# Attention with both heads of a pair together: scores in alternate row halves, values as weights of the sums, probabilities divided first

## The reference

```
def dilated_mixer(x, k_sh, v_sh, cos, sin, norm_g, w_q, q_norm_g, w_o):
    h = rms_norm(x, norm_g)
    q = (h @ w_q).reshape(Bn, Sn, N_GROUPS, HEADS_PER_GROUP, ATT_HEAD)
    q = apply_rope(rms_norm(q, q_norm_g[:, None, :]), cos, sin)
    for gi, (window, dilation) in enumerate(DILATED_GROUPS):
        o, l = dilated_window_attention(q[:, :, gi], k_sh[:, :, gi], v_sh[:, :, gi], window, dilation)
    ...
    alpha = jax.nn.softmax(jnp.stack(lses), axis=0)
    o = jnp.einsum('gbsh,gbshd->bshd', alpha, jnp.stack(outs))
    return o.reshape(Bn, Sn, O_WIDTH).astype(x.dtype) @ w_o
```

## Time and profile before

| | |
|---|---|
| median of 3 runs | 1139.49 us |
| lowest, highest | 1134.31, 1140.91 us |
| span of the profiled execution | 1131.1 us |
| TensorE, VectorE, ScalarE, GpSimd busy | 95%, 58%, 38%, 7% of the span |
| granted TensorE clock, mean | 0.975 |
| steps of the pairs in the trace | half 0 of pair 1 at 617.56 us, of pair 7 at 845.12, last step to 899.7 |
| DMA | 137.30 MB, mean 121 GB/s |

### The profile page before, as it was taken

One profiled execution on the slowest core, in us unless ns is written; L12 is line 12 of the kernel. 1 busy time (PEld: TensorE's weight loads), 2 busy tenths in 40 slices (PEclk: granted clock), 3 DMA queues, 4 the chain that ended last, 5 costly groups with the idle time before them and its releaser, 6 DMA issues.

```text
span 1131.1 us, 17783 instructions
## 1 busy us (share of the span) xinstructions
PE 1070.4 (95%) x6728; PEld 955.1 (84%) x6728; DVE 654.6 (58%) x1107; ACT 429.7 (38%) x643; POOL 78.4 (7%) x52
## 2 busy tenths in 40 slices
PE   5989999999998799999978999999999899999998
PEld 3779779789687699999968999999999638999997
DVE  6754654753764655455476766776677216555553
ACT  2311312321312443343244556655655503433431
POOL 0000000000000000000002211221122000000000
PEclk9989999999999899999989999999999898999999
DMA  9310050040130375676449444334432314766761
GB/s 291 116 48 1 1 160 1 11 148 1 40 110 1 94 218 173 183 199 174 129 129 288 120 132 139 111 113 137 139 111 74 112 37 139 196 167 191 196 170 56
DMA packets 194954, 137.30 MB, mean 121 GB/s; under 512 B 7261, under 2 KB 185949, under 8 KB 194794
## 3 DMA queue, kind: packets, MB, share of 16 engines
q1 hardware_dynamic: 194922, 136.85, 41.5%
HBM read 135.78 MB, written 1.05 MB: 121 GB/s over the span
## 4 chain that ended last, share of the span: by engine, by line
issue 55%; PE 36%; POOL 5%; DVE 2%; DMA 1%; ACT 1%; SPq 0%; POOLq 0%; DVEq 0%; ACTq 0%
PE bank L392 21%; PE wide L392 15%; POOL gsm L1448 5%; DMA ring<-in_w_kv 1%; DVE x L1045 0%; DVE wsp L1045 0%; DMA x<-in_x 0%; DVE fhn L1048 0%; POOL small L1448 0%; ACT once L798 0%; SPq L359 0%; DVE work L1045 0%; PE bank L402 0%; PE bank L744 0%; PE wide L402 0%
## 5 line engine op out<-in xcount | busy, mean ns | idle before, releaser
L392 PE MATMUL bank<-wpj,hkq 128*128 128x384 f32 x1152 | 217.2, 343 | 5.4 <-DVE wpj L1045 3.1
L392 PEld LDWEIGHTS bank<-wpj,hkq 128*128 128x128 f32 x1152 | 201.1, 190 | 12.0 <-issue 4.6
L1045 DVE TENSOR_TENSOR wsp<-ring,wsp 128x1024 fp32r<-128x1024 f32 (+1 forms) x88 | 151.0, 1756 | 34.0 <-ACT wsp L798 34.0
L798 ACT ACTIVATE wsp<-ring 128x1024 fp32r<-128x1024 f32 (+1 forms) x88 | 130.0, 1484 | 27.2 <-PE wide L392 27.2
L392 PEld LDWEIGHTS wide<-hsp,wsp 128*128 128x128 f32 x1056 | 133.2, 197 | 5.2 <-DVE hsp L1045 3.6
L392 PE MATMUL wide<-hsp,wsp 128*128 128x256 f32 x1056 | 134.1, 288 | 2.8 <-DVE hsp L1045 2.8
L392 PE MATMUL bank<-work 128*128 128x128 f32 (+4 forms) x896 | 130.6, 301 | 6.4 <-DVE work L1048 4.2
L392 PEld LDWEIGHTS bank<-hsp,wsp 128*128 128x128 f32 x1056 | 129.5, 192 | 1.6
L392 PE MATMUL bank<-hsp,wsp 128*128 128x256 f32 x1056 | 130.2, 283 | 0.0
L392 PEld LDWEIGHTS bank<-work 128*128 128x128 f32 (+2 forms) x896 | 117.0, 195 | 14.9 <-issue 5.8
L1448 POOL TENSOR_TENSOR gsm<-gsm,mhalf 128x6 f32<-128x6 f32 (+1 forms) x40 | 73.8, 1844 | 582.7 <-DVE gsm L1168 348.0
(11 more groups left out here) (155 smaller groups left out, 1197.8 us busy)
## 6 DMA issues: line engine op xcount, KB each, us to landing
ring<-in_f_w_gu SPq DMA_DIRECT2D x88, 512.0 KB, 5.6
ring<-in_w_kv SPq DMA_DIRECT2D x96, 256.0 KB, 3.3
ring<-in_f_w_down SPq DMA_DIRECT2D x44, 512.0 KB, 3.7
ring<-in_b_w_q SPq DMA_DIRECT2D x48, 256.0 KB, 3.5
wmix<-in_a_w_k SPq DMA_DIRECT2D x4, 1024.0 KB, 7.0
wmix<-in_a_w_r SPq DMA_DIRECT2D x4, 1024.0 KB, 10.3
wmix<-in_a_w_v SPq DMA_DIRECT2D x4, 1024.0 KB, 5.9
wmix<-in_a_w_o SPq DMA_DIRECT2D x4, 1024.0 KB, 5.0
```

Of the source, the lines that this page charges most:

```text
L392: return pe.matmul(o, a, b, start=start, stop=stop)
L798: return act.activation(o, i, f, **k)
L1045: return dve.tensor_tensor(o, a, b, op)
```

## The change

Both heads of a pair now go through each step together, one row tile after the other, so i = 2r + h.

- `scores(r)` issues the products of both heads in turn, head 0 in rows 0 to 63 of the array and head 1 in rows 64 to 127, into two places: banks 2 and 7 for r = 0, `wide` and the new `wide2` (banks 5 and 6) for r = 1.
- After the exponential VectorE divides the probabilities by their sum (`normalise`) before they are turned. `scale_out` and `turn_out` are gone, and so is `ao`.
- `turn_p` writes the turned probabilities over the scores. `copy_p` is one instruction for each head and row tile.
- `weigh(r)` has the values as weights (64 columns, head 0 into partitions 0 to 63, head 1 into 64 to 127) and the turned probabilities as the moving operand of 128 columns. The result is already turned, and `copy_o(r)` takes it to `oT`.
- Turned keys go to banks 7 and 2, turned queries to banks 3 and 5. `project_half(4)` is no longer split around the attention's steps.
- The loops over the pairs are written out.
- The tile `rows` is enlarged to hold the probabilities of r = 0, and there is a new tile for `pT` of r = 0.

```diff
-        bank += [ctx.enter_context(nc.psum_tensor(f"bank{i}", [P, 512], F32)) for i in range(5, 8)]
+        wide2 = ctx.enter_context(nc.psum_tensor("wide2", [P, 1024], F32))
+        bank += [wide2[:, 0:512], wide2[:, 512:1024]]
+        bank += [ctx.enter_context(nc.psum_tensor("bank7", [P, 512], F32))]
...
+        SCORES = ((bank[2][:, 0:384], bank[7][:, 0:384]), (wide[:, 0:768], wide2[:, 0:768]))
+        OUT = (bank[2][:, 384:512], bank[7][:, 384:512])
+        QK = ((bank[7], bank[2]), (bank[3], bank[5]))
...
+                def scores(r):
+                    if r == 0:
                         pe.wait_ge(S("act_qkT"), b * 4 + 4)
+                        if b > 0:
+                            pe.wait_ge(S("act_oT"), b * 2)
+                    n = (r + 1) * P
                     for g in range(NG):
+                        for h in range(2):
+                            hp = slice(h * HD, (h + 1) * HD)
+                            m = mm(SCORES[r][h][:, g * n:(g + 1) * n], qTt[hp, g, r * P:(r + 1) * P], kTt[hp, g, 0:n])
+                            if g == NG - 1:
+                                m.then_inc(S("pe_s"), 1)
+
+                def turn_p(r):
+                    for h in range(2):
+                        pe.wait_ge(S("dve_pn"), b * 4 + (2 * r + h + 1))
+                        for j in range(NG * (r + 1)):
+                            m = pe.transpose(SCORES[r][h][:, j * P:(j + 1) * P], pr[r][:, h, j * P:(j + 1) * P], ident)
+                        m.then_inc(S("pe_pT"), 1)
+
+                def weigh(r):
+                    pe.wait_ge(S("act_pT"), b * 4 + (2 * r + 2))
+                    if r == 1 and p is not None:
+                        pe.wait_ge(S("act_qkT"), p * 4 + 1)
                     n = NG * (r + 1)
                     for j in range(n):
                         g, s = j // (r + 1), j % (r + 1)
+                        for h in range(2):
+                            m = mm(OUT[r][h * HD:(h + 1) * HD, :], Vs[:, s, g * P + h * HD:g * P + (h + 1) * HD],
+                                   pT[r][:, h, j * P:(j + 1) * P], j == 0, j == n - 1)
+                    m.then_inc(S("pe_o2"), 1)
...
                 if A: project_half(0)
-                if B: score(0); score(1)
+                if B: scores(0)
                 if A: project_half(1)
-                if B: turn_p(0); score(2)
+                if B: scores(1)
                 if A: project_half(2)
-                if B: turn_p(1); weigh(0); score(3)
+                if B: turn_p(0)
                 if A: project_half(3)
-                if B: turn_p(2); weigh(1)
-                if A: turn_qk(0, 0); turn_qk(0, 1); project_half(4, [0])
-                if B: turn_p(3); weigh(2)
-                if A: project_half(4, [1])
-                if B: weigh(3)
+                if B: weigh(0); turn_p(1)
+                if A: turn_qk(0, 0); turn_qk(0, 1); project_half(4)
+                if B: weigh(1)
                 if A: project_half(5)
                 if A: turn_qk(1, 0); turn_qk(1, 1)
-                if B: turn_out()
...
+                def copy_p(r, h):
+                    act.wait_ge(S("pe_pT"), b * 4 + (2 * r + h + 1))
+                    A(pT[r][:, h, :], SCORES[r][h], ACT.Copy).then_inc(S("act_pT"), 1)
...
+                def copy_o(r):
+                    act.wait_ge(S("pe_o2"), b * 2 + (r + 1))
+                    A(oT[:, b, r * P:(r + 1) * P], OUT[r], ACT.Copy).then_inc(S("act_oT"), 1)
...
                 if X: half_hi(p, 2)
-                if B: probs(0)
-                if X: copy_raw(0, 0); square(0, 0); copy_raw(0, 1)
-                if B: probs(1)
-                if X: square(0, 1); half_hi(p, 3)
-                if B: copy_p(0)
+                if B: probs(0, 0); probs(0, 1)
+                if X: copy_raw(0, 0); square(0, 0); copy_raw(0, 1); square(0, 1); half_hi(p, 3)
+                if B: probs(1, 0); probs(1, 1)
                 if X: half_hi(p, 4)
-                if B: probs(2); copy_p(1)
+                if B: copy_p(0, 0); copy_p(0, 1)
                 if X: copy_raw(1, 0); square(1, 0); copy_raw(1, 1)
-                if B: copy_p(2); probs(3)
-                if X: square(1, 1); half_hi(p, 5)
-                if X: copy_qk(0, kTt)
-                if B: copy_p(3)
+                if B: copy_o(0); copy_p(1, 0); copy_p(1, 1)
+                if X: square(1, 1); half_hi(p, 5); copy_qk(0, kTt)
                 if X and follow: half_hi(p + 1, 0)
-                if B: scale_out()
+                if B: copy_o(1)
                 if X: copy_v(0); copy_v(1); copy_qk(1, qTt)
...
+                def normalise(r):
+                    dve.wait_ge(S("act_p"), b * 4 + (2 * r + 2))
+                    dve.reciprocal(asm[:, 12 + 2 * r:14 + 2 * r], asm[:, 8 + 2 * r:10 + 2 * r]).then_inc(S("dve_rden"), 1)
+                    dve.wait_ge(S("dve_rden"), b * 2 + (r + 1))
+                    for h in range(2):
+                        i = 2 * r + h
+                        dve.tensor_scalar(pr[r][:, h, :], pr[r][:, h, :], asm[:, 12 + i:13 + i], None, ALU.mult).then_inc(S("dve_pn"), 1)
...
-                if B: mask_max(0)
-                if X: half_lo(p, 2)
-                if B: mask_max(1)
-                if X: mean_squares(0, 0); norm_rotate(0, 0); mean_squares(0, 1); half_lo(p, 3); norm_rotate(0, 1)
-                if B: mask_max(2); mask_max(3)
-                if X: half_lo(p, 4); mean_squares(1, 0); norm_rotate(1, 0)
+                if B: mask_max(0, 0); mask_max(0, 1)
+                if X: half_lo(p, 2); mean_squares(0, 0)
+                if B: normalise(0)
+                if X: norm_rotate(0, 0); mean_squares(0, 1); half_lo(p, 3); norm_rotate(0, 1)
+                if B: mask_max(1, 0); mask_max(1, 1)
+                if X: half_lo(p, 4)
+                if B: normalise(1)
+                if X: mean_squares(1, 0); norm_rotate(1, 0)
                 if X: mean_squares(1, 1); half_lo(p, 5); norm_rotate(1, 1)
```

More of the change, by code:

```diff
@@ L95, in program @@
         gain = sb("gain", [P, 2, D])
-        rows = sb("rows", [NR, D])
+        rows = sb("rows", [P, D])
         par = sb("par", [P, KT, NR])
@@ L249, in program @@
         akr = once[:, 0:1536].rearrange("p (j n) -> p j n", j=4)
-        pr, pT = (once[:, 1536 * (i + 1):1536 * (i + 2)].rearrange("p (b n) -> p b n", b=2) for i in range(2))
+        pr1, pT1 = (once[:, 1536 * (i + 1):1536 * (i + 2)].rearrange("p (h n) -> p h n", h=2) for i in range(2))
+        pr0 = rows[:, 0:768].rearrange("p (h n) -> p h n", h=2)
         turned_qk = sbv("turned_qk", [P, 2 * NG * T])
@@ L285, in _ @@
             load_gain(0, ins["a_norm_g"][0])
-            sp.dma_start(rows[:, :], ins["rows"]).then_inc(s_rows, 16)
+            sp.dma_start(rows[0:NR, :], ins["rows"]).then_inc(s_rows, 16)
             for dst, n in ((w1s, "a_w1"), (a1s, "a_a1"), (g1s, "a_g1")):
@@ L715, in turn_qk @@
                     pe.wait_ge(S("dve_kr"), p * 4 + (2 * w + r + 1))
[L716 to L719, removed]
+                    if b is not None and w == 0 and r == 1:
+                        pe.wait_ge(S("act_oT"), b * 2 + 1)
                     for g in range(NG):
-                        m = pe.transpose(bank[5 + r][:, g * P:(g + 1) * P], akr[:, 2 * w + r, g * P:(g + 1) * P], ident)
+                        m = pe.transpose(QK[w][r][:, g * P:(g + 1) * P], akr[:, 2 * w + r, g * P:(g + 1) * P], ident)
@@ L731, in score @@
                     for g in range(NG):
[L732 to L745, removed]
@@ L785, in _ @@
             pe.wait_ge(s_wo, 16)
-            pe.wait_ge(S("act_oT"), KT)
+            pe.wait_ge(S("act_oT"), 2 * KT)
             for r in range(RT):
@@ L1396, in norm_rotate, with mask_max @@
                     tt(akr[:, j, :], am1.rearrange("p g h d -> p (g h d)"), am2.rearrange("p g h d -> p (g h d)"), ALU.add).then_inc(S("dve_kr"), 1)
[L1398 to L1400 removed]
+                def mask_max(r, h):
+                    i = 2 * r + h
                     dve.wait_ge(S("pe_s"), b * 4 + (i + 1))
[L1402 to L1403 removed]
                     dve.memset(asm[:, 48 + i:49 + i], 0.0)
[L1406 to L1407 removed]
+                    dve.tensor_tensor_reduce(pr[r][:, h, :], SCORES[r][h], C(f"mask{r}"), 1.0, 3.0 * NEG, ALU.add, ALU.max,
                                              asm[:, i:i + 1]).then_inc(S("dve_sm"), 1)
```

72 lines of the change are left out of this document (10 added, 62 removed).

## The result

The changed kernel takes 1150.53 us, the median of four runs (1146.61 to 1152.82); the kernel before, run beside it, 1139.94. The ratio is 1.0112, 95% interval 1.0081 to 1.0143. Forecast were 1156 us and a range of 1144 to 1174. The profiled execution took 1146.61 us (span 1144.8), the shortest of the four. The spans of the others are 1148.5 to 1151.0 at granted clocks of 0.958 to 0.953, against 0.963 here: the longer executions are those with the lower clock.

What follows compares the result with a forecast made beforehand. TensorE was taken as the bound, busy 95% of 1131.1 us. Seven pairs x (40.4 - 37.93) = 17.3 and the last pair -1.0 gave 16.3 us on 1139.5: 1156 us, range 1144 to 1174.

Steps and rivals of the forecast that it cites:

- Scores and sums: Products on TensorE in each pair: scores 2.1 us, 2.2 less than before; sums 2.3 us, 0.064 an instruction.
- the rival of serial columns: Sums on TensorE do not overlap, 0.107 to 0.128 us an instruction: 26 us more, 1166 us; chance 0.25.
- The chain to the copies: VectorE's masks, then ScalarE's exponentials and copies pT0, end at 24.3 us of a pair; TensorE waits 4.2 at weigh(0).
- The divisions: VectorE's new divisions of the probabilities: 0.55 us for 384 columns, 0.95 for 768, 0.9 where the next follows at once.
- a pair without slow clock: New pair of 39.2 us before any clock loss, 1.3 more than 37.93; as a rival 1148 us, chance 0.12.
- The clock: TensorE's granted clock falls behind the wait: 1.2 us a pair, ends 0 and 2.0, giving 40.4 a pair.
- The root of GpSimd: GpSimd's root in each pair, 1.32 us when VectorE is quiet; the forecast did not have the divisions hold it up.
- the rival's case: VectorE's divisions hold up GpSimd's root, making everything after it 1.0 us later in each pair: 1163 us; chance 0.08.
- Last step: The last pair, with nothing to project beside it: 15.1 us against 16.6, taken as 1 us less, ends -3 and +1.
- The rival of a faster kernel: No wait forms at weigh(0) and TensorE stays the bound: pair 34.0 us, 29 us less, 1111 us; chance 0.05.
- The level: Whole kernel before: median of three runs 8.4 us above the span of 1131.1, kept as the base of 1139.5 us.

Runs made afterwards that it cites:

- e6: The changed kernel with the same steps in another order on TensorE, ScalarE and VectorE: 1110.19 us, ratio 0.9769 to the kernel before.
- e8: e6 with the sums of head 0 first, then those of head 1, no longer alternating: 1117.06 us, ratio 0.982 to the kernel before.
- e1: The changed kernel with half_hi(4) and the copies pT0 moved ahead of probs(1,0) and probs(1,1) on ScalarE: 1127.57 us, ratio 0.9923 to the kernel before.
- e2: The changed kernel with 16 unused float32 products a pair added on TensorE behind half 3: 1138.3 us, ratio 1.0027 to the kernel before.
- e3: The kernel before with its loops over pairs written out, nothing else: 1134.48 us, ratio 0.999 to the kernel before.
- e5: The changed kernel again, unedited, on another chip: 1154.28 us, ratio 1.0147 to the kernel before.
- e7: e6 with the scores of head 0 first, then those of head 1: 1113.42 us, ratio 0.9802 to the kernel before.
- e11: e6 with one row tile of the following half between the two heads' scores: 1128.53 us, ratio 0.9936 to the kernel before.
- e4: The changed kernel with the scores of head 0 first, then those of head 1: 1152.47 us, ratio 1.013 to the kernel before.

## Why the prediction was right

**Scores and sums.** Forecast 2.1 us a pair for the scores, measured 0.87 + 1.50 = 2.4; sums forecast 2.3, measured 0.81 + 1.46 = 2.3 at a granted clock of 1.00 (e6). That the column halves overlap, taken from the row halves alone, e8 showed; the rival of serial columns falls (0.061 to 0.068 us an instruction, not 0.107).

**The chain to the copies.** From the start of half 0 (735.62): first mask forecast 5.3, measured 5.35; second masks 18.7, measured 18.96; end of probs(1,1) 22.0, measured 22.15; copies' end 24.3, measured about 24.4; wait forecast 4.2, measured 4.00. This reading from one pair of before was the step that carried the forecast, and e1 showed that ScalarE's order makes the wait.

**The divisions** were priced too high: 0.617 us for 768 columns and 0.416 for 384 over the loop pairs, where I took 0.95 and 0.55 (mean of 14 each, 600 to 900 us):

```profile
L1389 DVE TENSOR_SCALAR once<-once,gsm 128x768 f32<-128x768 f32 x14 | 8.0, 617 | 0.2
...
L1389 DVE TENSOR_SCALAR rows<-rows,gsm 128x384 f32<-128x384 f32 x14 | 5.2, 416 | 0.3
```

The slope of the earlier trace rows to half_lo's was no guide: between the two lengths it is 0.52 ns a column, half of the 1.05 taken. So turn_p(1) waited 0.22 us in this pair and 0.9 at most, not 1.2 (from 25.0 to 26.2); and a pair without slow clock is 38.8 us (e2) instead of 39.2.

**The clock** was priced too low: 2.0 us a pair (e2), the upper end of the bounds, not 1.2. The two errors cancel in part: a settled pair is 40.8 us against 40.4. The first pairs were shorter: from one weigh(0) to the next it is 39.5 us, 40.2, and then 40.6 to 40.9. Over the seven pairs the sum is 19.3, against 17.3, so the pairs cost more than forecast.

**The root of GpSimd** was not held up: it starts at 745.20, beside the divisions at 745.22, and lasts 1.32 us as with a quiet VectorE; norm_rotate waits 0.58 for it. Inside half_lo's addition it lasts 2.76, as before.

```profile
745.20 1.32 POOL L1421 TENSOR_TENSOR gsm<-gsm,mhalf 128x6 f32<-128x6 f32 x1 [15.53 <-DVE gsm L1356]
...
749.58 2.76 POOL L1421 TENSOR_TENSOR gsm<-gsm,mhalf 128x6 f32<-128x6 f32 x1 [3.07 <-DVE gsm L1356]
```

The Trainium skill, "SBUF — State Buffer", section "Who interferes with whom", says of a tensor_scalar in a two-port mode and a GpSimd instruction that the one issued first keeps the shared ports and the other is blocked. These rows don't agree, if the divisions run in such a mode: the root started 0.02 us ahead, and both divisions behind it were over at 745.97, inside its 1.32 us, the first in 0.42 us and the second in 0.41. What a division that is ahead of the root does to it, the rival's case, they do not test: in every pair of every traced version that divides the root is ahead.

**Last step and what lies outside the pairs.** The last step was forecast 1.0 us shorter and measured 0.6. From the 16.3 forecast, 2.0 go on top for the pairs and 0.4 for the last step; 3.1 come off for the earlier start of pair 1 and 2.6 for the projection, and 0.7 go on top behind it: 13.7. The forecast held both stretches outside the pairs as unchanged. They differ between executions of the same work, as e3 and e5 show, so it is luck that the span came out under the forecast while the pairs came out over it.

**The rival of a faster kernel** needed the chain 2.5 us shorter a pair. I had put it at 0.05, rightly for this order; e1 takes 3.2 us off a pair (37.6 from 721.40 to 759.01) by two calls in another place, and is 0.8% faster than the kernel before.

**The level.** I carried over 8.4 us between span and median; in the changed kernel the median lies 5.7 above the profiled span, as that execution was the shortest. Those 2.7 us and the 2.6 between 16.3 and 13.7 are 5.3 of the 5.5 by which the forecast is too high. Against the kernel before run beside it, the forecast of 16.3 us more is 1.4%; the two comparisons gave 1.1% and 1.5% (e5). What was right is the mechanism: the place of the wait, its releaser, its length within 0.2 us, and the clock falling behind it.

## What to carry to other kernels

When TensorE is the bound, work taken off it is worth its time only if every operand is early enough for the new order: e6 does the same work as the changed kernel and takes 3.8% less time on the same chip (1110.19 against 1154.28 us in e5), by the order of the queues alone. Follow the chain of the other engines to each operand, from the point at which TensorE releases it, and count what stands ahead in each queue, whether or not it has to do with the operand. A wait of a few microseconds that comes back in each round can cost its clock as well, here 2.0 us for one of 4.0; if the wait can't go, it is worth trying to fill it with work, which here made the kernel faster (1.0027 of the time before against 1.0112).

## What the hardware showed that I had not expected

- Blocks of instructions in different row halves overlap in part even when they don't alternate: 3.2 us in two blocks (e7), 2.4 alternating, 4.7 apart (e11).
- A TENSOR_SCALAR with a scalar per partition from SBUF to SBUF goes at 0.52 ns a column between 384 and 768 columns of float32, while mask and maximum on 768 columns from PSUM take 0.952 us.
- In e4 the pairs alternate, weigh(0) starting at 679.58, 721.55, 761.45, 803.43, 843.32 and 883.75: 42.0 us, 39.9, 42.0, 39.9 for the same instructions, and then 40.4. In the long ones the twelve transposes and half 4 take 2.82 and some 5.5 us, in the short ones 2.3 and 4.4. In the changed kernel the pairs are all 40.6 to 40.9 from the third on. With e1, where one wait of 2.41 us in seven was followed by no slow clock, it shows that what the clock takes from a pair depends on more than the length of its wait; why stays open.
